# Reordering the hand-over from the first token mixer to the first MLP in a two-layer diffusion trunk kernel

## What is computed

```python
for i in range(2):                       # mixer 0: pooling, mixer 1: short gated convolution
    sh_m, sc_m, gt_m, sh_f, sc_f, gt_f = split(silu(c) @ ada_w[i] + ada_b[i], 6)
    h = modulate(rms_norm(x, norm_g[i, 0]), sh_m, sc_m)
    y = pool_mixer(h, pool_w, pool_scale) if i == 0 else short_conv_mixer(h, ...)
    x = x + gt_m * rms_norm(y, norm_g[i, 1])
    hf = modulate(rms_norm(x, norm_g[i, 2]), sh_f, sc_f)
    x = x + gt_f * rms_norm(square(relu(hf @ ffn_w1[i])) @ ffn_w2[i], norm_g[i, 3])
```

## Time and profile before

| | |
|---|---|
| median of three runs | 974.17 us (972.28 to 974.63) |
| the profiled execution | 976.7 us, its span 974.6 us |
| PE busy | 957.4 us, 98% of the span |
| DVE, ACT busy | 532.4 us, 334.1 us |
| mean granted clock of PE | 0.993 of full |

### The profile page before, as it was taken

How to read it: one execution, slowest core, us unless ns; L and a number is a source line. 1 busy time by engine, 2 the same in 40 slices (tenths; PEclk the granted TensorE clock), 3 DMA queues, 4 the chain that set the end, 5 groups by cost and what they waited for, 6 DMA issues and landing times.

```text
span 974.6 us, 11463 instructions
## 1 busy us (share of the span) xinstructions
PE 957.4 (98%) x4791; PEld 789.4 (81%) x4791; DVE 532.4 (55%) x598; ACT 334.1 (34%) x437; POOL 35.7 (4%) x70
## 2 busy tenths in 40 slices
PE   8889999999999999999999999999999999999997
PEld 6658888888888888889888888988888888888886
DVE  6686464553465446686766546755455324433444
ACT  6554422331243134264222323542143114313422
POOL 3002000010001001000101000000000000000000
PEclk9899999999999999999999999999999999999999
DMA  9997273345334444314656431254423332233201
GB/s 306 304 352 260 85 256 130 130 170 182 130 130 167 173 141 156 125 62 177 200 173 238 156 108 44 89 194 164 158 87 108 103 114 87 87 98 119 87 22 65
DMA packets 80587, 144.66 MB, mean 148 GB/s; under 512 B 3950, under 2 KB 33746, under 8 KB 80536
## 3 DMA queue, kind: packets, MB, share of 16 engines
q1 hardware_dynamic: 78376, 139.52, 42.2%
q0 software_dynamic: 2160, 4.41, 1.3%
HBM read 141.79 MB, written 2.13 MB: 148 GB/s over the span
## 4 chain that ended last, share of the span: by engine, by line
PE 94%; DMA 2%; DVE 2%; issue 1%; ACT 1%; POOL 0%; DVEq 0%; SPq 0%; POOLq 0%
PE ps L416 30%; PE ps L418 30%; PE ps L417 29%; DMA win<-in_ada_w_dram 1%; PE ps L612 1%; DMA raw<-in_ada_w_dram 1%; PE ps L619 1%; PE ps L527 1%; PE ps L647 0%; DVE w_parts L1081 0%; PE ps L690 0%; PE ps L445 0%; PE ps L638 0%; DVE y L1151 0%; PE ps L632 0%
## 5 line engine op out<-in xcount | busy, mean ns | idle before, releaser
L1081 DVE TENSOR_TENSOR w_parts<-raw,w_parts 128x2048 fp32r<-128x2048 f32 x81 | 185.6, 2292 | 258.4 <-ACT w_parts L837 258.4
L416 PE MATMUL ps<-in_hi,w_parts 128*128 128x512 f32 (+1 forms) x784 | 290.0, 370 | 0.9 <-DVE in_lo L1162 0.5
L417 PE MATMUL ps<-in_lo,w_parts 128*128 128x512 f32 (+1 forms) x784 | 288.0, 367 | 0.0
L418 PE MATMUL ps<-in_hi,w_parts 128*128 128x512 f32 (+1 forms) x784 | 288.0, 367 | 0.0
L837 ACT ACTIVATE w_parts<-raw 128x2048 fp32r<-128x2048 f32 x81 | 154.7, 1911 | 387.8 <-PE ps L418 386.8
L416 PE MATMUL ps<-w_parts,mid_hi 128*128 128x512 f32 x576 | 224.4, 390 | 0.0
L418 PE MATMUL ps<-w_parts,mid_lo 128*128 128x512 f32 x576 | 224.1, 389 | 0.0
L417 PE MATMUL ps<-w_parts,mid_hi 128*128 128x512 f32 x576 | 224.1, 389 | 0.0
L416 PEld LDWEIGHTS ps<-in_hi,w_parts 128*128 128x128 f32 x784 | 147.7, 188 | 29.2 <-issue 3.3
L418 PEld LDWEIGHTS ps<-in_hi,w_parts 128*128 128x128 f32 x784 | 147.8, 188 | 24.6
L417 PEld LDWEIGHTS ps<-in_lo,w_parts 128*128 128x128 f32 x784 | 147.8, 189 | 24.1
(11 more groups left out here) (152 smaller groups left out, 469.2 us busy)
## 6 DMA issues: line engine op xcount, KB each, us to landing
raw<-in_ffn_w_dram SPq DMA_DIRECT2D x64, 1024.0 KB, 5.1
ada_raw<-in_ada_w_dram SPq DMA_DIRECT2D x56, 512.0 KB, 5.5
raw<-in_conv_in_w_dram SPq DMA_DIRECT2D x16, 512.0 KB, 4.9
raw<-in_ada_w_dram SPq DMA_DIRECT2D x4, 1024.0 KB, 11.0
ada_sum<-in_ada_w_dram SPq DMA_DIRECT2D x4, 1024.0 KB, 12.9
win<-in_ada_w_dram SPq DMA_DIRECT2D x4, 1024.0 KB, 11.9
raw<-in_conv_in_w_dram SPq DMA_DIRECT2D x4, 1024.0 KB, 5.5
raw<-in_conv_out_w_dram SPq DMA_DIRECT2D x4, 1024.0 KB, 5.4
```

What stands on the lines that cost most here:

```text
L416: nc.tensor.matmul(o, hi, b_hi, start=start, stop=False)
L417: nc.tensor.matmul(o, hi, b_lo, start=False, stop=False)
L418: return nc.tensor.matmul(o, lo, b_hi, start=False, stop=stop)
L1081: nc.vector.tensor_tensor(w_lo[:, u % W_SLOTS, :], raw[:, u % RAW_SLOTS, :], w_hi[:, u % W_SLOTS, :].bitcast(F32), ALU.subtract).then_inc( ...
```

## The change

Between the last pooling products and the end of unit 1's parts, the orders on all four engines are rewritten:

- SP: pieces 10 and 11 (the last two gate quarters) are loaded ahead of unit 1.
- Unit 1's high and low parts are made in two halves, at two places in ACT's and DVE's orders. `part(side, 0)` needs the first half alone.
- The gates of quarters 2 and 3 are applied for one side at a time, the second side's between the tiles of the first.
- `first_x(2)`, `first_x(3)` and their norms move behind the first side's inputs.
- PE makes both parts of side 0 first, then both of side 1. `add_up(14)` moves ahead of `turn_up(8)` and the first turns. `part(1, 1)` moves from behind `second_unit(3)` to before `add_up(18)`.

```diff
@@ SP
-            for i in range(2, 10):
+            for i in range(2, PRE_F):            # PRE_F = 12
                 load_pre(i)
             load(1)
-            for i in range(10, PRE_F + 6):
+            for i in range(PRE_F, PRE_F + 6):
                 load_pre(i)
@@ PE
             add_up(PRE_F + 1)
             stay_busy(0, 6)
+            add_up(PRE_F + 2)
             turn_up(8)
...
                 turn_first(0, 0)
-                add_up(PRE_F + 2)
                 turn_first(0, 2)
                 add_up(PRE_F + 3)
+                turn_first(0, 1)
+                turn_up(9)
                 part(0, 0)
+                turn_first(0, 3)
                 add_up(PRE_F + 4)
+                part(0, 1)
+                add_up(PRE_F + 5)
                 turn_first(1, 0)
-                turn_first(0, 3)
-                add_up(PRE_F + 5)
-                turn_up(9)
+                turn_up(10)
                 turn_first(1, 2)
-                turn_up(10)
-                turn_first(0, 1)
+                turn_first(1, 1)
                 part(1, 0)
                 turn_first(1, 3)
+                part(1, 1).then_inc(unit_done, 1)
                 add_up(PRE_F + 6)
-                turn_first(1, 1)
-                part(0, 1)
                 add_up(PRE_F + 7)
                 pe.wait_ge(f_lo, 4)
+                pe.wait_ge(xt_copied, len(FIRST_COPIED))
                 second_unit(2)
                 turn_up(11)
                 second_unit(3)
-                part(1, 1).then_inc(unit_done, 1)
@@ ACT
+            def first_unit_hi(h):
+                act.wait_ge(raw_in[1], raw_value(1))
+                cols = slice(h * 2 * UN, (h + 1) * 2 * UN)
+                nc.scalar.activation(w_hi[:, 1, cols], raw[:, 1, cols], ACT.Copy).then_inc(w_hi_ready if h else first_half_hi, 1)
...
-            split_hi(1)
+            first_unit_hi(0)
             group_squares(2)
+            first_unit_hi(1)
             group_squares(3)
...
             copy_sums(8)
+            first_hi(0)
+            copy_sums(9)
+            copy_first(0, 2)
+            first_hi(1)
+            copy_first(0, 3)
             first_root(2)
-            first_hi(0)
-            copy_first(0, 2)
             first_root(3)
-            copy_sums(9)
-            copy_first(0, 3)
             copy_sums(10)
-            first_hi(1)
-            split_hi(2)
             first_hi(2)
             copy_first(1, 2)
+            first_hi(3)
+            split_hi(2)
             copy_first(1, 3)
-            first_hi(3)
             split_hi(3)
@@ DVE
             group_gate(0)
-            split_lo(1)
+            first_unit_lo(0)
             group_out(3)
             group_gate(1)
             gate_copy(2)
+            gate_copy(3)
...
-            gate_copy(3)
-            group_gate(2)
+            group_gate(2, 0)
+            group_gate(3, 0)
             dve.wait_ge(y0_rms, 1)
             nc.vector.reciprocal(st0[:, 4, :], st0[:, 3, :]).then_inc(y0_rcp, 1)
-            group_gate(3)
             first_x(0)
             first_x(1)
-            first_x(2)
+            group_gate(2, 1)
             first_norm(0)
+            group_gate(3, 1)
             first_norm(1)
             columns(8)
             first_input(0)
             first_lo(0)
+            first_unit_lo(1)
+            columns(9)
+            first_input(1)
+            first_x(2)
+            first_lo(1)
             first_x(3)
             first_norm(2)
             first_norm(3)
-            first_input(1)
-            columns(9)
-            first_lo(1)
             first_input(2)
+            columns(10)
+            first_lo(2)
+            first_input(3)
+            first_lo(3)
             split_lo(2)
-            first_lo(2)
-            columns(10)
-            first_input(3)
             first_input(4)
-            first_lo(3)
             first_lo(4)
```

More of the change, by code:

```diff
@@ L176, in trunk @@
         gate_in, a_in, sh_in = sem("gate_in"), sem("a_in"), sem("sh_in")
+        first_half_hi, first_half_lo = sem("first_half_hi"), sem("first_half_lo")
         w_hi_ready, w_lo_ready, unit_done, bank_done = sem("w_hi_ready"), sem("w_lo_ready"), sem("unit_done"), sem("bank_done")
@@ L295, in wait_pos @@
                 eng.wait_ge(s, value)
-        FIRST_TURNED = ((0, 0), (0, 2), (1, 0), (0, 3), (1, 2), (0, 1), (1, 3), (1, 1))
+        FIRST_TURNED = ((0, 0), (0, 2), (0, 1), (0, 3), (1, 0), (1, 2), (1, 1), (1, 3))
         FIRST_COPIED = ((0, 2), (0, 3), (1, 2), (1, 3))
-        FIRST_MADE = ((0, 0), (1, 0), (0, 1), (1, 1), 2, 3)
-        FIRST_BANK = {(0, 0): 6, (1, 0): 6, (0, 1): 6, (0, 2): 7, (0, 3): 7, (1, 2): 7, (1, 3): 7, (1, 1): 7}
+        FIRST_MADE = ((0, 0), (0, 1), (1, 0), (1, 1), 2, 3)
+        SIDE_GROUPS = (2, 3)
+        GATED = GROUPS + len(SIDE_GROUPS)
         def first_part(side, pair):
@@ L307, in first_turn @@
         def first_turn(side, pair):
-            return ps[:, FIRST_BANK[side, pair], :].rearrange("p (n t) -> p n t", n=2)
+            return ps[:, 6 + pair // 2, :].rearrange("p (n t) -> p n t", n=2)
         def edges(w):
@@ L678, in turn_first @@
                 pe.wait_ge(x1_norm, 2 * side + 2)
[L679 to L684, removed]
+                pe.wait_ge(y0_gated, GATED)
+                if pair < 2:
+                    wait_pos(pe, f_made, FIRST_MADE.index((side, pair)))
                 else:
@@ L698, in part @@
                     pe.wait_ge(f_lo, FIRST_MADE.index((side, pair)) + 1)
-                    need_weights(1)
+                    if pair == 0:
+                        pe.wait_ge(first_half_lo, 1)
+                    else:
+                        need_weights(1)
                     for k in (2 * pair, 2 * pair + 1):
@@ L1081, in split_lo, with first_unit_lo @@
                 nc.vector.tensor_tensor(w_lo[:, u % W_SLOTS, :], raw[:, u % RAW_SLOTS, :], w_hi[:, u % W_SLOTS, :].bitcast(F32), ALU.subtract).then_inc(w_lo_ready, 1)
+            def first_unit_lo(h):
+                if h:
+                    dve.wait_ge(w_hi_ready, 2)
+                else:
+                    dve.wait_ge(first_half_hi, 1)
+                cols = slice(h * 2 * UN, (h + 1) * 2 * UN)
+                nc.vector.tensor_tensor(w_lo[:, 1, cols], raw[:, 1, cols], w_hi[:, 1, cols].bitcast(F32), ALU.subtract).then_inc(w_lo_ready if h else first_half_lo, 1)
             def add_ada(i):
@@ L1359, in group_out, with group_gate @@
                                         ALU.mult).then_inc(y0_copied, 1)
-            def group_gate(g):
+            def group_gate(g, side=None):
                 dve.wait_ge(ada_turned, 4 + g + 1)
-                gate = ps[:, 6 + g % 2, 0:Q].unsqueeze(1).to_broadcast([P, NT, Q])
                 dve.wait_ge(y0_sq, NT * (g + 1))
-                nc.vector.tensor_tensor(y_tok[:, :, quarter(g)], y_tok[:, :, quarter(g)], gate, ALU.mult).then_inc(y0_gated, 1)
+                tiles = slice(0, NT) if side is None else slice(2 * side, 2 * side + 2)
+                gate = ps[:, 6 + g % 2, 0:Q].unsqueeze(1).to_broadcast([P, tiles.stop - tiles.start, Q])
+                nc.vector.tensor_tensor(y_tok[:, tiles, quarter(g)], y_tok[:, tiles, quarter(g)], gate, ALU.mult).then_inc(y0_gated, 1)
             def first_x(t):
                 dve.wait_ge(y0_rcp, 1)
-                dve.wait_ge(y0_gated, GROUPS)
+                dve.wait_ge(y0_gated, GROUPS if t < 2 else GATED)
                 nc.vector.scalar_tensor_tensor(out=xs[:, t, :], in0=y_tok[:, t, :], scalar=st0[:, 4, t:t + 1], in1=xs[:, t, :],
```

## The result

The changed kernel takes 976.08 us in the median of seven runs (975.81 to 978.33). The kernel before, run beside it, takes 973.96 (972.28 to 974.63). The ratio is 1.0027, 95% interval 1.0018 to 1.0037: 2.1 us slower by the medians, 2.6 by the ratio, a small loss but clear of the noise. The prediction said 973.4. The profiled execution of the changed kernel took 975.88 us with a span of 973.8, 0.8 us *less* than the profiled execution of before (span 974.6). This contradiction is the centre of the case: the two profiles alone say "faster", the medians say "slower".

What follows compares the result with a forecast made beforehand. PE, busy 98% of the span, was taken as the bound. Terms of -0.9, -1.0, +1.05 and +0.1 sum to -0.75 us, giving 973.4 on the median of 974.2, range 971.0 to 976.5.

Steps and rivals of the forecast that it cites:

- the new wait: ACT and DVE wait for unit 1's first half until 53.5 us, so `group_out(3)` starts at 55.7 instead of 54.61: +1.1 us.
- The loads: SP's queue: unit 1, issued near 44.05 behind pieces 10 and 11, lands near 53.5, 4.2 us later than before.
- The gain of the early pieces: SP's queue no longer runs dry: piece 12 lands at 56.4, piece 13 at 59.4, 3.3 us earlier than before.
- From `group_out(3)` to `first_x(0)`: DVE's gates by sides: 6.28 us becomes 5.1, by -1.1 for half gates and -0.1 for `gate_copy(3)` moved ahead.
- PE late for side 0: PE started the first turn 0.86 us after DVE was ready; with early pieces it starts at 66.25, not 67.15: -0.9 us.
- Piece 14 ahead: `add_up(14)` runs before the first turn on PE and is out of the way behind it: -1.0 us.
- the holes of 0.1 and 1.05: PE idle between first turns and parts: 0.1 us on side 0 and 1.05 us on side 1.
- The hole on side 1: PE stops at `turn_first(1, 1)` for `f_made` and `part(1, 0)` for `f_lo`, with no `add_up` to fill: +1.05 us.
- That unit 1 is not late: Rival, chance 0.2: unit 1 lands where it did, giving -2.3 us, 971.9, or 970.9 with a filled hole or full clock.
- That unit 1 lands later still: Rival, chance 0.1: unit 1 lands a us or more later, side 1's norms miss their 0.4 us; 974.5 to 975.
- The clock rival: Rival, chance 0.28: PE's clock falls to 1.2 GHz in the new holes, at 66 us; 975.1 (0.18) or 976.7 (0.1).

Runs made afterwards that it cites:

- experiment 1: The kernel before, unchanged, run and profiled once more: 973.02 us, ratio 0.9996; profiled execution 972.96 us, span 970.9.
- the first of experiment 2: The kernel before with one edit, pieces 10 and 11 loaded ahead of unit 1: 978.58 us, ratio 1.0057.
- that of 3: The changed kernel, new load order kept, with unit 1's high halves and first low half moved later, no gate work behind that wait: 975.48 us, ratio 1.0014.
- the last of 4: The changed kernel, new load order kept, with ten unread products before pieces 12 and 13 and piece 14's sum behind the first turn: 978.15 us, ratio 1.0045.
- the kernel with filler in the holes: The changed kernel with old load order, piece 14's sum behind the first turn, ten unread products before pieces 12 and 13: 974.59 us, ratio 1.0017.
- experiments 2 to 4: Kernels with load order changed alone or undone, unit 1's halves later, or PE's filler and piece 14 rearranged: ratios 1.0014 to 1.0057.
- that pair: Pieces 12 to 19 loaded by half, filler before pieces 12 and 13: changed kernel (old load order, piece 14 behind) 974.24 us; kernel before 973.85 us.

## Why the prediction was wrong

**The step that failed** is the one from the sum on one profile to the time, and in the sum the term of the new wait, "+1.1 us", that was sized on the same profile. The prediction's words: "-0.75 us on the span of 974.6 (profiled time 976.7, so 975.9); on the median of 974.2 it is 973.4". The sum held for the execution that it was made on: the spans differ by 0.8 us, and the profiled time of the changed kernel is 975.88. In part that was luck, as the two misses named above cancel. But that execution of before carried a stretch of over 6 us at 1.2 GHz in the pooling products, and a second one from 62.9 us, neither of which experiment 1 has; its span is 3.7 us shorter. The prediction saw the signs, the stretches and the 2.5 us between profiled time and median, and subtracted the 2.5 us from both kernels, as if the changed kernel would lose them too on a usual run. It does not: against experiment 1 the new wait is +3.57 us and the changed kernel ends 2.9 us later.

The landing of unit 1 tells why. In the old load order it moves with the time of its issue, which waits for PE: issued at 44.05 behind the slow stretch it lands at 49.25, issued at 40.3 to 41.0 in the eight profiles without such a stretch in front it lands at 46.8 to 47.8. In the new order it ends a row of transfers that follow each other without a gap, and lands at 52.75 to 53.06 in all four profiles (the changed kernel, the first of experiment 2, that of 3 and the last of 4). An early PE then waits. That a late PE would find it at the same time is argued and not shown: none of these four profiles has the early slow stretch. The times fit it: all seven runs of the changed kernel but one lie within 975.8 and 976.8.

**The terms, against the usual execution.** The loads: unit 1 lands 11.9 us after issue, predicted as to mechanism and nearly to size (53.5 for 52.75). The gain of the early pieces was sized 3.3 us from a queue that "ran dry". It did in the earlier trace rows (4.5 us from piece 9 to unit 1), but in experiment 1 unit 1 lands 2.8 us behind piece 9, PE meets piece 12 at 56.55 and piece 13 at 59.57, and the predicted 56.4 and 59.4 are no gain. In the changed kernel piece 12 lands at 55.65, 0.9 us earlier, and PE comes to it only at 59.78. The new wait: "+1.1 us" was sized against a `group_out(3)` held back to 54.61 by the slow stretch; against 51.41 it is +3.57. From `group_out(3)` to `first_x(0)` it is 5.71 us for 6.28, and 5.1 was predicted. The 5.71 hold 0.65 and 0.16 of waits for gate turns at 1.2 GHz, and 4.9 without them; the kernel with filler in the holes, at full clock, has 5.37 with a wait of 0.54 for the sum of piece 11 in it. PE late for side 0: the -0.9 does not exist, since in experiment 1 PE waits 0.36 us for DVE. Piece 14 ahead, with the holes of 0.1 and 1.05: -1.0 us and +1.15 were to give +0.15 from the first turn to `second_unit(0)`; it is -0.1 (29.15 us for 29.25). From the first turn to `part(0, 0)` PE takes 3.14 us for 3.44. The hole on side 1: 0.83 for 1.05, nearly balanced by the steps that left that stretch (26.01 us for 25.81).

**The rivals.** That unit 1 is not late is refuted (6.0 us of waiting). That unit 1 lands later still is refuted. The clock rival was put at 66 us; the low clock came earlier, from just before 55 to past 61 us. It begins in the hole of 5.1 us and slows two gate turns (2.08 us) and a part of the pieces' sums. DVE waited 0.65 and 0.16 us for those turns, so it cost at most 0.8 us here. In the profiles of experiments 2 to 4 in which filler and piece 14 ran at 1.2 GHz in front of the first turn it cost more.

**What is shown, and what is not.** Shown: the load order alone costs 5.1 us in the kernel before and 3.6 between two otherwise equal changed kernels. Shown too: it is not the only cause, since the changed kernel with the old load order is hardly faster (975.86 for 976.08). Shown by the timelines: with the wait removed, PE's filler, the moved sum and low clock take its place, and with these mended the pieces and the two steps in front of `part(0, 0)` leave +1.16. The granted clocks of all executions say how often the clock stays up: of 98 of the kernel before 42 had 0.998 or more (median 973.0, the others 974.0), of the 30 of the four kernels with the new load order none. Not shown: what the filler costs by itself, and how much a faster stream of pieces would be worth, since the clock moved in both kernels of that pair.

## What to carry to other kernels

Before a sum is made, compare the profiled execution's time with the median: if they differ by more than the effect that is forecast, find the stretch that makes the difference and ask whether the change keeps it. A transfer put ahead in a full queue delays each one behind it, and a copy that waits for such a one delays all later work of its engine, also work that does not need it: here one late unit became waits of 6.0 us on ACT, 5.1 on DVE and 5.1 on PE. In this stage DVE's chain, PE's queue with its clock and the stream of pieces end within a few us of each other; each time one was shortened, another took its place.

## What the runs showed of the hardware

The slow stretches move from execution to execution of one kernel: in the kernel before at 35 and 63 us in one profile and nowhere in another (mean granted clock 1.0). Of its 87 times beside the experiments, from 971.9 to 976.3 us, those below 973 have a mean granted clock of 0.998 or 0.999 in 18 of 26 cases, and those above 974.5 have 0.991 to 0.995 in 14 of 17. In the changed kernels with the old load order, or with the unit's halves later, the clock fell at or behind the two waits for pieces 12 and 13, with the six unread products in place (between 58 and 61 us, three profiles) and without them (at 61 us, one profile). With ten of them in the waits it was at full there in all five profiles with the old load order, but in three of these it fell later, and the kernel before did not gain by them. 16 sum products take 1.07 us at full clock and 1.93 at 1.2 GHz. Loads of 1 MB in a full queue land 2.8 to 3.0 us apart.
